# Sample value products of the differential attention heads, with the values as moving operand in four column groups

## The reference, cut to what matters

```
a = p[:, :, 0] - lam * p[:, :, 1]
return (jnp.einsum('bhqk,bkhe->bqhe', a[..., :P], v_past.astype(F32))
        + jnp.einsum('bhqk,bkhe->bqhe', a[..., P:], v.astype(F32)))
...
y = o * lax.rsqrt(jnp.mean(o * o, axis=-1, keepdims=True) + EPS) * g.astype(F32) * (1.0 - lam_init)
```

## Time and profile before

| what | value |
| --- | --- |
| median of three runs | 3354.06 us |
| profiled execution: its own time | 3355.46 us |
| span of its instructions | 3353.9 us |
| TensorE matmul busy | 3180.0 us, 95% of the span |
| VectorE, ScalarE, GpSimd busy | 39%, 23%, 5% |
| mean granted TensorE clock | 0.959 of full speed |
| attention heads | about 411 to 931 us in the span |

### The profile page before, as it was taken

The page is one execution under the profiler, slowest core; times in us unless marked ns, Lnnn a source line. Parts: engine busy times, 40 slices in busy tenths (PEclk is TensorE's granted clock), DMA queues, the critical chain, the costliest instruction groups (busy, mean ns, idle before and its releaser), DMA issues.

```text
span 3353.9 us, 54834 instructions
## 1 busy us (share of the span) xinstructions
PE 3180.0 (95%) x22657; PEld 3078.9 (92%) x22657; DVE 1295.9 (39%) x1818; ACT 775.4 (23%) x839; POOL 172.3 (5%) x278
## 2 busy tenths in 40 slices
PE   6999999988999999878899999999999999999996
PEld 5999988988989899767799999999999999999996
DVE  6444244243354444622733232332323223232336
ACT  5111122122122223312421221211212122121221
POOL 1000111211211100000000000000000000000001
PEclk8999998998999999977999999999999999999998
DMA  5433433433545644142142222323222222223241
GB/s 194 120 105 107 143 112 112 136 119 114 171 151 163 228 142 147 53 113 59 68 115 84 80 88 75 86 76 87 78 85 76 87 78 85 82 81 88 75 144 56
DMA packets 401373, 357.29 MB, mean 107 GB/s; under 512 B 9806, under 2 KB 364224, under 8 KB 399248
## 3 DMA queue, kind: packets, MB, share of 16 engines
q1 hardware_dynamic: 379520, 270.16, 27.3%
q0 software_dynamic: 21776, 86.10, 7.5%
HBM read 306.81 MB, written 49.41 MB: 106 GB/s over the span
## 4 chain that ended last, share of the span: by engine, by line
PE 86%; DVE 5%; issue 3%; ACT 1%; DMA 1%; DVEq 0%; POOLq 0%; POOL 0%; ACTq 0%; SPq 0%
PE gemm L1725 76%; PE aux L1800 1%; DVE yT L1514 1%; PE aux L1878 1%; PE gemm L2106 1%; ACT w_hi L799 1%; DVE yT L1706 1%; PE aux L1904 1%; PE gemm L1768 1%; DMA d_kp<-in_cache_diff_k 1%; PE aux L1854 1%; PE aux L2004 0%; DVE w_lo L1113 0%; PE aux L1990 0%; PE aux L2087 0%
## 5 line engine op out<-in xcount | busy, mean ns | idle before, releaser
L1725 PE MATMUL gemm<-act_hi,w_hi 128*128 128x288 f32 x4608 | 1019.2, 303 | 6.9 <-DVE act_lo L1523 4.3
L1725 PE MATMUL gemm<-act_lo,w_hi 128*128 128x288 f32 x4608 | 996.6, 298 | 0.0
L1725 PE MATMUL gemm<-act_hi,w_lo 128*128 128x288 f32 x4608 | 995.7, 298 | 0.0
L1725 PEld LDWEIGHTS gemm<-act_hi,w_hi 128*128 128x128 f32 x4608 | 753.3, 192 | 31.4 <-DVE act_lo L1523 14.2
L1725 PEld LDWEIGHTS gemm<-act_lo,w_hi 128*128 128x128 f32 x4608 | 753.3, 192 | 0.0
L1725 PEld LDWEIGHTS gemm<-act_hi,w_lo 128*128 128x128 f32 x4608 | 751.5, 191 | 0.0
L1113 DVE TENSOR_TENSOR w_lo<-w_raw,w_hi 128x2048 fp32r<-128x2048 f32 x216 | 494.6, 2290 | 238.3 <-ACT w_hi L799 115.6
L1725 PE MATMUL gemm<-u_lo,w_hi 128*128 128x288 f32 x2048 | 438.8, 296 | 0.0
L1725 PE MATMUL gemm<-u_hi,w_hi 128*128 128x288 f32 x2048 | 438.8, 296 | 0.0
L1725 PE MATMUL gemm<-u_hi,w_lo 128*128 128x288 f32 x2048 | 438.7, 296 | 0.0
L1725 PEld LDWEIGHTS gemm<-u_lo,w_hi 128*128 128x128 f32 x2048 | 330.4, 189 | 0.0
(11 more groups left out here) (293 smaller groups left out, 2085.7 us busy)
## 6 DMA issues: line engine op xcount, KB each, us to landing
w_raw<-in_w_mlp_up SPq DMA_DIRECT2D x64, 1024.0 KB, 6.4
w_raw<-in_w_mlp_down SPq DMA_DIRECT2D x64, 1024.0 KB, 5.7
w_raw<-in_w_in SPq DMA_DIRECT2D x56, 1024.0 KB, 5.8
w_raw<-in_w_out SPq DMA_DIRECT2D x16, 1024.0 KB, 5.7
z_scratch<-z_out SPq DMA_DIRECT2D x56, 288.0 KB, 2.1
r_zin<-z_scratch POOLq DMA_DIRECT2D x8, 1152.0 KB, 6.1
xin<-in_x_prompt POOLq DMA_DIRECT2D x8, 1024.0 KB, 5.4
d_kp<-in_cache_diff_k POOLq DMA_DIRECT2D x64, 128.0 KB, 2.5
```

The costliest lines, as they stand in the source:

```text
L1725: ins = M(out[half][:, 0:TH], w[b][:, cols], x[:, k, half * TH:(half + 1) * TH], start=first and n == 0, stop=last and n == 2)
```

## The change

The products of the samples swap their operands. The stationary operand is now 32 columns of d_ats, of which 8 are the sample's weights and the others are not used; the moving one is a page of values with all its 256 columns. The result has tokens on partitions. Sample j of a group of four writes partitions 32j to 32j+31 of one bank, with its own column group of the array (tile_position). There are two groups of four samples, in A[2] and A[3], each with two pages and the new positions, so 12 products in a group and 24 in a head.

A group waits for the pages of all its four samples. GpSimd loads all the pages of the second group after the step og0, which ends the first group. Quarters 21 and 22 both stand between the groups. VectorE copies each group's result to SBUF (d_ot); after quarter 23 TensorE turns them back with four transposes into A[1], and VectorE copies the wanted columns into d_o (os0, os1). d_ats gets 32 more columns and is cleared once before the heads; d_diag, which nothing uses, is gone.

```diff
-        d_ats = sb("d_ats", [P, NPG + 1, TS], F32, st)
+        d_ats = sb("d_ats", [P, NPG + 1, TS + 32], F32, st)
+        d_ot = sb("d_ot", [P, 2, 2 * P], F32, st)
...
+                pool.wait_ge(D_PE.sem, D_PE.of("og0", h))
+                pool.sem_inc(s_idle, 1)
                 for b in range(4, DB):
-                    pool.wait_ge(D_PE.sem, D_PE.of(f"os{b - 4}", h))
-                    pool.sem_inc(s_idle, 1)
                     value_page(h, b)
...
                 tile_end(5)
-                after(D_PE, "os7", h)
-                dve.wait_ge(D_DVE.sem, D_DVE.before("os0", h))
-                D_DVE.did(V.tensor_copy(d_o[:, 0, TP:T], A[2][:, 0:TS]), "os0")
-                dve.wait_ge(D_DVE.sem, D_DVE.before("os1", h))
-                D_DVE.did(V.tensor_copy(d_o[:, 1, TP:T], A[3][:, 0:TS]), "os1")
+                for g in range(2):
+                    after(D_PE, f"og{g}", h)
+                    dve.wait_ge(D_DVE.sem, D_DVE.before(f"ot{g}", h))
+                    D_DVE.did(V.tensor_copy(d_ot[:, g, :], A[2 + g][:, 0:2 * P]), f"ot{g}")
+                after(D_PE, "ot", h)
+                for e in range(2):
+                    dve.wait_ge(D_DVE.sem, D_DVE.before(f"os{e}", h))
+                    D_DVE.did(V.tensor_copy(d_o[:, e, TP:T].rearrange("p (b q) -> p b q", q=DS),
+                                            A[1][:, 2 * e * P:2 * (e + 1) * P].rearrange("p (b r) -> p b r", r=32)[:, :, 0:DS]), f"os{e}")
                 tile_end(6)
 
+            V.memset(d_ats[:], 0.0).then_inc(d_zero, 1)
+            dve.wait_ge(d_zero, 1)
             for h in range(DH):
                 d_head(h)
...
-                for b in range(DB):
-                    pe.wait_ge(d_vin[b % 4], h * (2 * 16 * NPG) + 16 * NPG * (b // 4 + 1))
-                    for e in range(2):
-                        if b == 0:
-                            M(A[2 + e][:, 0:TS], d_kv[0:TS, PC, 2 + e, :], d_ats[0:TS, NPG, :], start=True, stop=False, skip_group_check=True)
-                        for n in range(NPG):
-                            ins = M(A[2 + e][:, b * DS:(b + 1) * DS], d_vk[b % 4][:, n, e, :], d_ats[:, n, b * DS:(b + 1) * DS],
-                                    start=False, stop=b == DB - 1 and n == NPG - 1, skip_group_check=True)
-                    D_PE.did(ins, f"os{b}")
-                    if b in (1, 4):
-                        fill(21 + b // 4)
+                for g in range(2):
+                    for j in range(4):
+                        pe.wait_ge(d_vin[j], h * (2 * 16 * NPG) + 16 * NPG * (g + 1))
+                    for n in range(NPG + 1):
+                        for j in range(4):
+                            b = 4 * g + j
+                            rows, values = (P, d_vk[j][:, n, :, :]) if n < NPG else (TS, d_kv[0:TS, PC, 2:4, :])
+                            ins = M(A[2 + g][32 * j:32 * j + 32, 0:2 * P], d_ats[0:rows, n, b * DS:b * DS + 32],
+                                    values.rearrange("p e d -> p (e d)"), start=n == 0, stop=n == NPG, tile_position=(0, 32 * j))
+                    D_PE.did(ins, f"og{g}")
+                    if g == 0:
+                        fill(21, 22)
                 fill(23)
+                after(D_DVE, "ot1", h)
+                for e in range(2):
+                    for g in range(2):
+                        ins = turn(A[1][:, (2 * e + g) * P:(2 * e + g + 1) * P], d_ot[:, g, e * P:(e + 1) * P])
+                D_PE.did(ins, "ot")
                 after(D_ACT, "sq", h)
```

More of the change, by code:

```diff
@@ L229, in program @@
         d_p = [sb(f"d_p{m}", [P, TP], F32, st) for m in range(2)]
-        d_diag = [sb(f"d_diag{m}", [P, P], F32, st) for m in range(2)]
         d_kp = [sb(f"d_kp{b}", [P, NPG, 2, P], F32, st) for b in range(2)]
@@ L404, in program @@
         D_DVE = Steps(sem("d_dve"), " ".join(dn)
-                      + " o0 o1 st smask snm sbias sr srl dsel ats atn os0 os1")
+                      + " o0 o1 st smask snm sbias sr srl dsel ats atn ot0 ot1 os0 os1")
         D_ACT = Steps(sem("d_act"), " ".join(f"kv{c}" for c in range(NT)) + " " + " ".join(f"exp{s}" for s in range(8))
@@ L411, in program @@
             f"s{s}" + (f" at{s}" if s % 2 else "") for s in range(8)) + " o0 o1 kt0 " + " ".join(
-            f"kt{b + 1} st{b}" for b in range(DB - 1)) + " st7 sT sn aT " + " ".join(f"os{b}" for b in range(DB)) + " ss sss")
+            f"kt{b + 1} st{b}" for b in range(DB - 1)) + " st7 sT sn aT og0 og1 ot ss sss")
         d_in = sem("d_in")
@@ L418, in program @@
         d_free = sem("d_free")
+        d_zero = sem("d_zero")
         d_kvfree = sem("d_kvfree")
@@ L1349, in d_head @@
                 dve.wait_ge(D_DVE.sem, D_DVE.before("ats", h))
-                D_DVE.did(V.tensor_copy(d_ats[:, 0:NPG, :].rearrange("p n t -> p (n t)"), A[0][:, 256:256 + NPG * TS]), "ats")
+                D_DVE.did(V.tensor_copy(d_ats[:, 0:NPG, 0:TS], A[0][:, 256:256 + NPG * TS].rearrange("p (n t) -> p n t", t=TS)), "ats")
                 dve.wait_ge(D_DVE.sem, D_DVE.before("atn", h))
-                D_DVE.did(V.tensor_copy(d_ats[0:TS, NPG, :], A[0][0:TS, 256 + NPG * TS:256 + (NPG + 1) * TS]), "atn")
+                D_DVE.did(V.tensor_copy(d_ats[0:TS, NPG, 0:TS], A[0][0:TS, 256 + NPG * TS:256 + (NPG + 1) * TS]), "atn")
                 tile_end(5)
-                after(D_PE, "os7", h)
-                dve.wait_ge(D_DVE.sem, D_DVE.before("os0", h))
-                D_DVE.did(V.tensor_copy(d_o[:, 0, TP:T], A[2][:, 0:TS]), "os0")
-                dve.wait_ge(D_DVE.sem, D_DVE.before("os1", h))
-                D_DVE.did(V.tensor_copy(d_o[:, 1, TP:T], A[3][:, 0:TS]), "os1")
+                for g in range(2):
[7 more added lines that the diff above has]
+                                            A[1][:, 2 * e * P:2 * (e + 1) * P].rearrange("p (b r) -> p b r", r=32)[:, :, 0:DS]), f"os{e}")
                 tile_end(6)
+            V.memset(d_ats[:], 0.0).then_inc(d_zero, 1)
+            dve.wait_ge(d_zero, 1)
             for h in range(DH):
```

## The result

The changed kernel takes 3368.82 us (median of 16 runs, 3360.39 to 3377.36), the kernel before 3357.23 (16 runs, 3350.27 to 3366.64). The ratio is 1.0035, with a 95% interval of 1.0024 to 1.0046: slower by 0.35%, 11.6 us. Forecast were 3368 us and +0.4%.

What follows compares the result with a forecast made beforehand. TensorE bounds the kernel, with 86% of the chain of waits. The stretches add 10.5 us and a later clock fall 3.6, +14.1 on the profiled 3355.46: 3369.6; the median is 1.4 lower, so 3368 us, range 3357 to 3388.

Steps and rivals of the forecast that it cites:

- Products side by side: Sample value products: four column groups work at once, 1.25 us plus 0.25 for switches, 1.5 us a group.
- Rival B: Sample value products: groups don't run side by side, 5.0 + 0.25 us each, 3398 us; two side by side, 3378; chance 0.13.
- Release to the first DMA: After the first group's products: 0.15 us to its result, then 1.34 to GpSimd's first page DMA.
- Seven steps: GpSimd's eight page DMAs for samples 4 to 7: first to eighth start, 8.8 us in three heads, 8.46 in the fourth.
- Landing: The last page DMA of samples 4 to 7 lands 2.40 us after its start.
- Idle 6.2 us in every head: Ahead of the second group: TensorE, with only quarters 21 and 22 as cover, waits 6.2 us for pages.
- Clock behind it: Second group and quarter 23, after the page wait: 4.7 us at 1.2 GHz, costing 2.35 us a head.
- End of the turn: Behind quarter 23: transposes, copies and Square come before the first sum of squares, 2.4 us, TensorE idle for 1.8.
- A second fall of the clock: After the idle 1.8 us before the sums: 3.6 us at half clock costs 1.8, in half of the heads, +3.6.
- The forecast for the stretches: First value product to first sum of squares, four heads: 95.05 us together against 84.52, +10.5.
- the drain at a change of tiling mode: Within a group, between 128-row and 64-row products: TensorE drains; switches there and at the end add 0.25 us.
- The estimate from the 2.38 times for three column tiles: A group's products: 1.6 us in place of 1.25, about 0.3 us more a group, 3 us in all.

Runs made afterwards that it cites:

- e5: The kernel before, with unswapped products, given separate buffers for the value pages of samples 4 to 7; 3346.19 us, ratio 0.9970 to the kernel before.

## Why the prediction was right

The mechanism was right, step by step, and most terms of the sum were too. Two were off, in opposite directions.

- **Products side by side, 1.5 us a group:** 1.57. Rival B (5.25 us one after the other) was a fair one: another loop order comes to it, with 6.1 us.
- **Release to the first DMA, 0.15 + 1.34:** from quarter 21's start to the first DMA 1.77, 1.50, 1.77 and 1.43 us in the four heads, as in 512.26 to 514.03. **Seven steps, 8.8 and 8.46:** 8.60, 9.07, 8.60 and 8.04. The two together come to 40.8 us in four heads, as forecast. **Landing 2.40:** 2.30.
- **Idle 6.2 us in every head:** 6.16, 6.42, 6.16 and 5.39.
- **Clock behind it, 2.35 a head:** too small. The low clock lasted 4.0, 8.3, 8.3 and 5.8 us, a mean of 6.6 and not 4.7. At half of it, as the forecast prices a spell, that is 3.3 a head and 13.2 in all against 9.4. Half is a little too dear, though: TensorE's busy time for the same work, 66.45 us here and 54.41 at full clock with own buffers, gives 12.0, or 3.0 a head. Its rows came from three cases with other work behind the wait, and in two heads here the low spell was longer than in any of them.
- **End of the turn 2.4 us, 1.8 idle:** 2.37 from the transposes (531.70) to the sum (534.07), 1.77 idle in all heads.
- **A second fall of the clock behind these 1.8 us in half of the heads, +3.6:** it didn't come in any head of the changed kernel. In the run with own buffers it came in one of four. This term was too large by 3.6, where the one before was too small by 2.6. The earlier trace rows was one case and proved nothing on its own.

The forecast for the stretches was 95.05, with the fall behind them 98.65; measured are 97.67. That the whole came out so close is partly luck: two errors of 2.6 and 3.6 us stood against each other. With both terms as measured the forecast would have been 13.1 us, slower by the same mechanism. The 13.2 us of the stretches and the medians' 11.6 agree within the scatter of the runs.

The account of the runs, by sums of the four stretches: freeing the pages of the kernel before is worth 7.9 us (84.5 to 76.6); the swap then 15.1 (to 61.5); the release as the change has it, with a group's joint wait and the low clock behind it, costs 36.2 (to 97.7). Together +13.2. Not seen in the forecast was that the old products are followed by a spell of half clock even without a wait, 3.4 us in each head of e5, which costs up to half of that, 1.7 us a head. It was inside the old stretches' times, so it did not spoil the sum.

The two rules of the Trainium skill: on the drain at a change of tiling mode ("TensorEngine Tiling (Array Packing)", Key Properties) the trace agrees, with 0.3 us in a group of 1.57 beyond its 1.25 of columns. The estimate from the 2.38 times for three column tiles ("TensorE: Matmul & The Clock Gate", Measured speedup vs the span model), 1.6 us for the rounds, was too high for the page products: rounds of four records start 0.22 us apart (510.70, 510.93), close to the 0.21 of their columns.

## What to carry to other kernels

Ask of a faster step what it releases and how late: here a gain of 15 us became a loss of 13 because four samples' buffers came free at once behind it, and eight DMAs at 1.2 us each then stood in one row on one queue. Price such a wait as the series of issues plus one landing, less the work beside it, and add the clock behind it. Put products of different column groups, with the same rows, next to each other in the queue. A long row of products with few moving columns can be dear twice, by its own time and by the clock of what follows; quarters of a large product between them made 14 us less here.

## What the runs showed of the hardware that was not expected

- A stretch in which TensorE is never idle can still run at half clock for a part of it: the granted clock was 0.77 over 22.4 us with eight samples' small products in a row (8 moving columns each), 0.91 with quarters between them, 1.00 with the swapped ones.
- Four column groups with 256 float32 columns each ran almost without loss: twelve products in 1.57 us, against 6.1 in the order sample after sample.
- The same instructions of the cross-attention took 116.9 to 130.5 us over nine profiles of nine kernels, none of which changes them; at 119.8 and 130.5 the clock was 0.65 and 0.58. A single profile's span can be off by as much as the effect that is looked for.
